# The input projection of a decoder layer as seven block products, with one order of events for all engines

## The reference

```
h = rms_norm(x, norm1_g) * (1 + scale1) + shift1          # 1024 features
proj = h @ w_in                                            # 1024 x 2560
q, k, v, u, vg = split(proj)                               # 512 columns each
q = rms_norm(q per head of 64, q_norm_g); k = rms_norm(k per head, k_norm_g)
u = gelu(u); vn = rms_norm(gelu(vg) per group of 128, v_norm_g)
o_mlp = u * (tril(w_s) @ vn per chunk of 128 tokens + b_s)
```

## Time and profile before

| what | value |
|---|---|
| median of 3 runs | 3535.37 us (3531.87 to 3537.59) |
| profiled execution | 3530.1 us, span 3528.4 us |
| TensorE busy over the span | 3294.7 us (93%) |
| DVE, ACT, POOL busy | 1684.9, 1080.3, 1494.9 us |
| mean granted TensorE clock | 0.97 of full speed |
| bytes moved | 536.85 MB, 152 GB/s |

### The profile page before, as it was taken

One profiled execution on the slowest core, in us unless ns is written; L12 is line 12 of the kernel. 1 busy time (PEld: TensorE's weight loads), 2 busy tenths in 40 slices (PEclk: granted clock), 3 DMA queues, 4 the chain that ended last, 5 costly groups with the idle time before them and its releaser, 6 DMA issues.

```text
span 3528.4 us, 52997 instructions
## 1 busy us (share of the span) xinstructions
PE 3294.7 (93%) x17710; PEld 2288.5 (65%) x17711; DVE 1684.9 (48%) x2542; ACT 1080.3 (31%) x2337; POOL 1494.9 (42%) x1222
## 2 busy tenths in 40 slices
PE   4799999989999959999998999998999999899999
PEld 1344444436656637777776777776777778777777
DVE  0211212138878825554543553544555354566565
ACT  0221222238889812322210331220232121132220
POOL 0010110126656625554533654543555454565553
PEclk8899999989999979999999999999999999999999
DMA  8411101020110056777777667778677674322222
GB/s 327 164 33 59 54 30 49 30 82 2 49 50 14 2 186 213 247 236 242 254 250 274 210 228 245 235 243 267 220 237 241 225 242 154 103 79 77 72 84 78
DMA packets 237935, 536.85 MB, mean 152 GB/s; under 512 B 26831, under 2 KB 60351, under 8 KB 217705
## 3 DMA queue, kind: packets, MB, share of 16 engines
q1 hardware_dynamic: 207081, 361.36, 31.2%
q10 hardware_dynamic: 30592, 172.24, 13.9%
HBM read 498.96 MB, written 34.55 MB: 151 GB/s over the span
## 4 chain that ended last, share of the span: by engine, by line
PE 54%; DVE 6%; issue 2%; DMA 1%; ACT 1%; SPq 0%; DVEq 0%; ACTq 0%
PE ff_pB L1392 46%; PE s_pZ L962 3%; PE s_pO L976 3%; DVE ff_conv L1672 1%; DVE s_left L1038 1%; DMA ff_act_in<-scratch_catT 1%; DVE ff_x L1599 0%; DVE ff_act_in L1688 0%; PE s_pZ L968 0%; DVE s_stop L1042 0%; ACT ff_conv L1470 0%; DVE ff_conv L1674 0%; DVE ff_rs L1681 0%; DMA s_kpage<-in_cache_k 0%; DVE s_kpage L1665 0%
## 5 line engine op out<-in xcount | busy, mean ns | idle before, releaser
L1392 PE MATMUL ff_pB<-ff_act_in,ff_w 128*128 128x256 f32 (+1 forms) x2496 | 616.3, 391 | 38.4 <-DMA ff_act_in<-scratch_catT 18.4
L1392 PEld LDWEIGHTS ff_pB<-ff_act_in,ff_w 128*128 128x128 f32 x2496 | 474.2, 193 | 150.6 <-issue 64.7
L1727 POOL TENSOR_TENSOR ff_sums<-ff_w 128x512 f32<-128x512 f32 (+1 forms) x152 | 191.4, 1259 | 755.1 <-PE ff_pB L1392 609.6
L417 PE MATMUL in_pA<-in_w,in_hT 128*128 128x512 f32 (+1 forms) x1024 | 449.2, 594 | 1.0 <-DVE in_hT L536 1.0
L1672 DVE SCALAR_TENSOR_TENSOR ff_conv<-ff_raw,k_vecT,ff_conv 128x512 f32<-128x512 f32 x352 | 381.7, 1085 | 84.4 <-ACT ff_raw L1477 78.2
L1392 PE MATMUL ff_pB<-ff_diff_up,ff_sums 128*128 128x256 f32 (+1 forms) x1600 | 391.0, 387 | 26.7 <-DVE ff_x L1599 22.7
L1599 DVE SCALAR_TENSOR_TENSOR ff_x<-ff_pB,k_mod,ff_x 128x256 f32<-128x256 f32 (+2 forms) x448 | 213.9, 480 | 385.2 <-PE ff_pB L1392 382.1
L856 POOL TENSOR_TENSOR at_stop<-at_stop,at_left 128x512 f32<-128x512 f32 (+3 forms) x320 | 311.5, 999 | 181.4 <-ACT at_stop L796 176.0
L1500 ACT ACTIVATE ff_raw<-ff_pB 128x256 f32<-128x256 f32 (+1 forms) x352 | 136.0, 388 | 778.9 <-PE ff_pB L1392 772.9
L1392 PEld LDWEIGHTS ff_pB<-ff_diff_up,ff_sums 128*128 128x128 f32 x1600 | 301.8, 191 | 92.1 <-DVE ff_x L1599 23.5
L1648 DVE TENSOR_TENSOR ff_raw<-ff_raw,ff_pB 128x256 f32<-128x256 f32 (+1 forms) x264 | 111.4, 424 | 483.4 <-PE ff_pB L1392 483.3
(11 more groups left out here) (187 smaller groups left out, 4711.2 us busy)
## 6 DMA issues: line engine op xcount, KB each, us to landing
ff_w<-in_w_units ACTq DMA_DIRECT2D x136, 1024.0 KB, 6.0
s_kpage<-in_cache_k SPq DMA_DIRECT2D x512, 256.0 KB, 3.9
s_vpage<-in_cache_v SPq DMA_DIRECT2D x512, 256.0 KB, 3.1
wada<-in_w_ada SPq DMA_DIRECT2D x8, 3072.0 KB, 11.5
ff_w<-in_w_units ACTq DMA_DIRECT2D x16, 768.0 KB, 5.3
in_w<-in_w_in SPq DMA_DIRECT2D x5, 2048.0 KB, 19.4
in_x<-in_x_prompt SPq DMA_DIRECT2D x16, 512.0 KB, 5.3
ff_act_in<-scratch_catT SPq DMA_DIRECT2D x4, 2048.0 KB, 14.5
```

What stands on the lines that cost most here:

```text
L417: last = pe.matmul(pA[0:R, m % 2, :], hT[:, kt, t * R:(t + 1) * R], w[:, kt, col:col + DSB], start=kt == 0, stop=kt == KT - 1)
L1392: last = pe.matmul(into, left[:, kt * P:(kt + 1) * P], right[:, kt, :], start=kt == 0 and p in (1, 2, 5), stop=kt == depth(j) - 1, skip_gr ...
L1727: pool.tensor_tensor(S3, A11, A21, ALU.subtract).then_inc(sums_ready, 1)
```

## The change

x comes as columns (`x_cols`, features on partitions, already an input of the last stage), so that the transposes of x go. The 2048 tokens are taken as 8 pairs of tiles. The root mean square is a sum over partitions: ACT squares half of the features of a pair (`nsq`), POOL folds 8 slices to 2 (`fold`), TensorE multiplies by ones (`stat`), and after both halves ACT takes the root, DVE the reciprocal (`invert`), POOL multiplies (`scale`), ACT modulates (`modulate`). All of this but the multiplication and sums runs a pair ahead.

For u, gate, q and k a pair's 256 x 1024 by 1024 x 512 product is cut into 2 x 2 blocks (token tile by half of the features; half of the features by half of the columns) and made of seven products of four 256-column matmuls each. Sums of token blocks (`sums`, POOL) are made for each pair; differences of weight blocks (`tdiff`, DVE) once, one of them in place of a weight block. Products 1, 6, 7, 4 add up in one PSUM bank and 2, 5, 3 in another; ACT copies products 1, 6, 5, 4 to SBUF as they stand in the bank (`take`), DVE adds 2, 7 and 3 to those copies (`add`). v stays as two banks of 512 columns for each pair. u has tokens on partitions now; `om` adds `b_s` and multiplies with u in one DVE instruction per tile and group, in place, and is transposed by TensorE (`turn`) before its store. Norm, square and gain work on two tiles (1024 columns) at once. The samples come between the seventh and the eighth pair and use plain products. One list of events (`in_events`) gives every engine its order; the loops are unrolled. `w_in` loads in the order u, gate, q, k, v; the `k_wd` copies stand behind the loads; `b_s` is loaded as a column for each token of a chunk.

```diff
-IN_COLUMNS = {"q": 0, "k": DSB, "u": 3 * DSB, "g": 4 * DSB, "v": 2 * DSB}
+IN_COLUMNS = {"u": 3 * DSB, "g": 4 * DSB, "q": 0, "k": DSB, "v": 2 * DSB}
...
+            "hT": ctx.enter_context(nc.sbuf_tensor("in_hT", [P, 2, KT, 2 * P], F32)),
+            "hs": ctx.enter_context(nc.sbuf_tensor("in_hs", [P, KT, S], F32)),
...
-            small(k["bs"][:].rearrange("p g c -> p (g c)"),
-                  a["b_s"][0].rearrange("g (a c) -> a (g c)", a=1).to_broadcast([P, G * P]))
+            small(k["bs"][:], a["bs_cols"])
+            for b in range(NSEQ):
+                small(k["bs_s"][TS * b:TS * b + TS, :], a["bs_cols"][0:TS, :])
...
+            x_cols = a["x_cols"].rearrange("(t p) q -> p t q", p=P)
+            sp.dma_start(nxt["hT"][:, 0, :, :], x_cols[:, :, 0:2 * P]).then_inc(nxt["x_loaded"][0], 16)
+            for kind, col in IN_COLUMNS.items():
+                src = a["w_in"][0].rearrange("(t p) n -> p t n", p=P)[:, :, col:col + DSB]
+                sp.dma_start(nxt["w"][:, :, col:col + DSB], src).then_inc(nxt["w_loaded"][kind], 16)
+                if kind == "u":
+                    sp.dma_start(nxt["hs"][:], x_cols[:, :, SEQ:SEQ + S]).then_inc(nxt["xs_loaded"], 16)
+                    sp.dma_start(nxt["hT"][:, 1, :, :], x_cols[:, :, 2 * P:4 * P]).then_inc(nxt["x_loaded"][1], 16)
             sp.wait_ge(ws_masked, 2)
             for b in range(NSEQ):
                 sp.dma_start(wd[TS * b:TS * b + TS, :, TS * b:TS * b + TS], wsT[0:TS, :, 0:TS]).then_inc(wd_loaded, 16)
-            for t in range(TT):
-                sp.dma_start(nxt["x"][:, t, :], a["x_prompt"][0, t * P:(t + 1) * P, :]).then_inc(nxt["x_loaded"][t], 16)
-            for kind, col in IN_COLUMNS.items():
-                src = a["w_in"][0].rearrange("(t p) n -> p t n", p=P)[:, :, col:col + DSB]
-                sp.dma_start(nxt["w"][:, :, col:col + DSB], src).then_inc(nxt["w_loaded"][kind], 16)
-            sp.wait_ge(small_loaded, 16 * (14 + 4 * TS))
+            sp.wait_ge(small_loaded, 16 * (14 + NSEQ + 4 * TS))
             sp.wait_ge(wd_loaded, 16 * NSEQ)
...
+def in_events():
+    events = [("nsq", 0, 0), ("fold", 0, 0), ("stat", 0, 0), ("nsq", 0, 1), ("fold", 0, 1), ("stat", 0, 1), ("root", 0), ("invert", 0),
+              ("scale", 0), ("modulate", 0), ("sums", 0), ("tdiff", "u")]
...
+                   *once(("tdiff", "q"), ("invert", SAMPLE)), m("g", 6), *ahead(("nsq", 0), ("fold", 0)), m("g", 5), *ahead(("stat", 0)),
...
+                   m("k", 7), ("hnorm", p, "q"), ("om", p), *ahead(("modulate",)), m("k", 3), ("turn", p, "om")]
...
+IN_ADDED = [product for product in IN_PRODUCTS if product[2] in (2, 7, 3)]
+IN_TAKEN = [product for product in IN_PRODUCTS if product not in IN_ADDED]
+def in_bank(p, kind, part):
+    second = part in (2, 5, 3) or (kind == "v" and part == 1)
+    return 2 * (IN_UNITS.index((p, kind)) % 2) + second
...
+            def multiply(p, kind, part):
+                product = (p, kind, part)
+                R, bank = size(p), pB[in_bank(*product)]
+                B11, B12, B21, B22 = weights_of(kind)
+                if IN_EARLIER[product]:
+                    drained(pe, IN_EARLIER[product])
+                if p in (0, SAMPLE) and part in (1, 0, "s"):
+                    pe.wait_ge(w_loaded[kind], 16)
...
+                A11, A12, A21, A22 = tokens_of(p)
+                S1, S2, S3, S4 = (ss[:, n, :, :] for n in range(4))
+                if kind == "u" and part in (1, 2):
+                    pe.wait_ge(h_ready, KT * p + (halfk if part == 1 else KT))
+                if kind == "u" and part == 6:
+                    pe.wait_ge(sums_ready, 4 * p + 4)
+                if kind == "v":
+                    for kt in range(KT):
+                        last = pe.matmul(bank[:], hT[:, p % 2, kt, P * part:P * part + P], w[:, kt, IN_COLUMNS["v"]:IN_COLUMNS["v"] + DSB],
+                                         start=kt == 0, stop=kt == KT - 1)
+                    last.then_inc(prod_done, 1)
+                    return
+                if p == 0 and part in (6, 7, 4):
+                    pe.wait_ge(diffs_ready, 4 * (IN_KINDS.index(kind)) + {6: 3, 7: 3, 4: 4}[part])
+                T2, T3, T4 = (tw[kind][:, n, :, :] for n in range(3))
+                left, right = {1: (A11, B11), 2: (A12, B21), 6: (S2, T2), 5: (S1, B12), 7: (S3, T3), 3: (S4, B22), 4: (A22, T4)}[part]
+                for kt in range(halfk):
+                    last = pe.matmul(bank[:, 0:HC], left[:, kt, :], right[:, kt, :], start=kt == 0 and part in (1, 2, 5), stop=kt == halfk - 1,
+                                     skip_group_check=part in (6, 7, 4, 3))
+                last.then_inc(prod_done, 1)
...
+                elif name == "stat":
+                    p, half = which
+                    if roots_before(p):
+                        pe.wait_ge(rooted, roots_before(p))
...
+                    else:
+                        pe.wait_ge(folded, 2 * nth("fold", p, half))
+                        last = pe.matmul(pS[:, 0:2 * P], k["ones"][:], sq[:, 0:2 * P], start=half == 0, stop=half == 1)
+                    last.then_inc(statted, 1)
...
+                elif name == "turn":
+                    p, use = which
+                    R = size(p)
+                    if use == "om":
...
+                        pe.wait_ge(gained, nth("gain", p, "k"))
+                    for t in range(tiles(p)):
+                        turn_waits((p, use, t))
+                        src = raw["u" if use == "om" else use]
+                        for r in range(HP):
+                            last = pe.transpose(pX[turn_bank((p, use, t))][:, r * R:(r + 1) * R], src[0:R, t, r * P:(r + 1) * P], k["ident"][0:R, 0:R])
+                        last.then_inc(turn_done, 1)
...
+            def take(p, kind, part):
+                product = (p, kind, part)
...
+                bank, into = pB[in_bank(*product)], raw[kind]
+                act.wait_ge(prod_done, prod(product))
...
+                    t, half = {1: (0, 0), 6: (0, 1), 5: (1, 1), 4: (1, 0)}[part]
+                    dst, src = into[:, t, HC * half:HC * half + HC], bank[:, 0:HC]
+                act.activation(dst, src, ACT.Copy).then_inc(taken, 1)
...
+                elif name == "nsq":
+                    p, half = which
+                    if IN_AT[event] > 1:
+                        act.wait_ge(statted, IN_AT[event] - 1)
+                    if reduced_before(event):
+                        act.wait_ge(hss_ready, reduced_before(event))
...
+                    else:
+                        act.wait_ge(x_loaded[p % 2], 16 * (p // 2) + 16)
+                        src = hT[:, p % 2, halfk * half:halfk * half + halfk, :].rearrange("p t q -> p (t q)")
+                        act.activation(sq[:], src, ACT.Square).then_inc(squared, 1)
...
+            def add(p, kind, part):
+                product = (p, kind, part)
+                t, half, ahead = {2: (0, 0, 1), 7: (1, 1, 5), 3: (0, 1, 6)}[part]
+                dve.wait_ge(prod_done, prod(product))
+                drained(dve, (p, kind, ahead))
+                dst = raw[kind][:, t, HC * half:HC * half + HC]
+                dve.tensor_tensor(dst, dst, pB[in_bank(*product)][:, 0:HC], ALU.add).then_inc(added, 1)
...
+                elif name == "tdiff":
+                    kind, n = which[0], 4 * IN_KINDS.index(which[0])
+                    B11, B12, B21, B22 = weights_of(kind)
+                    T2, T3, T4 = (tw[kind][:, i, :, :] for i in range(3))
+                    dve.wait_ge(w_loaded[kind], 16)
+                    for i, (into, one, two) in enumerate(((T3, B22, B12), (B12, B12, B11), (T2, B22, B12), (T4, B21, T2))):
+                        if i:
+                            dve.wait_ge(diffs_ready, n + i)
+                        dve.tensor_tensor(into, one, two, ALU.subtract).then_inc(diffs_ready, 1)
...
+                    tile = raw[kind][0:R, 0:tiles(p), :].rearrange("p n (h e) -> p (n h) e", e=e)
+                    dve.tensor_tensor(tile, tile, hrstd[0:R, 0:n].unsqueeze(2).to_broadcast([R, n, e]), ALU.mult).then_inc(normed, 1)
+                elif name == "om":
+                    p, R = which[0], size(which[0])
+                    bs = k["bs_s"] if p == SAMPLE else k["bs"]
+                    dve.wait_ge(gelued, nth("gelu", p, "u"))
+                    for t in range(tiles(p)):
+                        dve.wait_ge(turn_done, TURN_AT[p, "mix", t])
+                        for g in range(G):
+                            u = raw["u"][0:R, t, g * P:g * P + P]
+                            ins = dve.scalar_tensor_tensor(u, pX[turn_bank((p, "mix", t))][0:R, g * P:g * P + P], bs[0:R, g:g + 1], u, ALU.add, ALU.mult)
+                        ins.then_inc(om_ready, 1)
...
+                if name == "fold":
+                    pool.wait_ge(squared, nth("nsq", *which))
+                    pool.tensor_tensor(sq[:, 0:4 * P], sq[:, 0:4 * P], sq[:, 4 * P:8 * P], ALU.add).then_inc(folded, 1)
```

(72 more changed lines are left out.)

614 lines of the change are left out of this document (289 added, 325 removed).

## The result

The changed kernel takes 3569.52 us (median of 4 runs, 3565.23 to 3571.39); the kernel before, beside it, 3533.68 (3531.87 to 3537.59). The ratio is 1.0096, 95% interval 1.0081 to 1.0110. The forecast was 3543 with a range up to 3563: the direction was right, the size was too small by 26.5 us, and the time lies outside the range. The profiled execution has a span of 3569.7 us, 41.3 more than the one before.

What follows compares the result with a forecast made beforehand. TensorE's count of matmul columns was taken as the bound. 143.3 + 580.6 + 35.6 + 1.0 + 4.4 = 764.9 against 757.08, 7.8 us later, gave 3538 profiled and 3543 as median; own range 3534 to 3553, with rivals 3518 to 3563.

Steps and rivals of the forecast that it cites:

- start at full pace: Time from which TensorE runs as if at full pace: 24.8 us after the barrier (bounds 21 and 29), at 143.3.
- (a): TensorE's wait in front of the `om` transposes, for DVE's chain behind k7: 2.7 us in each of eight pairs.
- (b): TensorE's wait in front of the next pair's column sum, behind g6 and g5: 2.0 us, seven times.
- first pair's extra: An extra table load in the first pair, costing 1 us.
- tail: Stage end, from the last v through transposes, copies and last store to the attention's first load: 4.4 us.
- The barrier: Before the projection: `k_wd` copies behind all x and w loads delay its start to 118.5, 17 us later.
- The longer chain: Stage start: the first pair's dependent norm, scale, modulation and sums take 28.1 us; full pace counts from 24.8 after the barrier.
- The products: TensorE's work: products 1.73 us apart, 66.4 us per pair, samples 43.4, column sums 6.0; 580.6 us in all.
- The forecast's own sign: Sign in the new profile that the forecast is wrong: products standing further apart than 1.8 us.
- the waits were not covered: Denies the faster rival: DVE and ACT keep ahead, the pairs' 35.6 us of waits go, 3507 us; chance 0.2.
- the barrier was held: Denies the no-change rival: copies land beside queued weights, start 4.8 us earlier, 3538 us; chance 0.1.
- Clearly slower: Rival: POOL's second scale instruction holds DVE's normalisation of q, 2.5 us per pair, 20 us, 3563; chance 0.2.

Runs made afterwards that it cites:

- the copies early: Changed kernel with the block of `ws_masked` and the eight `k_wd` copies put back ahead of the x and w loads: 3558.6 us, 1.0051 of the kernel before.
- both moves: Changed kernel with the `om` transposes behind the first v bank and the next pair's first column sum behind g7: 3512.8 us, 0.9936 of the kernel before.
- om later: Changed kernel with only the `om` transposes moved, behind the first v bank instead of in front of it: 3533.7 us, 0.9990 of the kernel before.

## Why the prediction was right in kind and wrong in size

| step | forecast | measured |
|---|---|---|
| stage begins | 118.5 | 116.23 |
| start at full pace | 143.3 | 139.9 (-3.4) |
| work of TensorE without waits and falls | 580.6 | 586.6 (+6.0) |
| waits (a) and (b), first pair's extra | 36.6 | 33.3 (-3.3) |
| lower clock behind the waits | 0 | 20.3 (+20.3) |
| tail | 4.4 | 5.9 (+1.5) |
| attention's first load | 764.9 | 785.97 (+21.1) |

Of the 26.5 us by which the forecast missed the median, 21.1 lie ahead of this load; the other 5 lie behind it, inside the scatter. The rows other than the lower clock add up to +0.8 us, which is luck: each is off by 1.5 to 6.0 and their signs cancel.

*The barrier* was right: copies behind the loads hold it. The bounds were 113.7 to 124; with the copies early it is 107.55.

*The longer chain*: 23.7 us instead of 24.8. POOL's two scale instructions took 6.47 (forecast 7.1, bounds 5.1 and 10).

*The products* are 1.73 us apart as forecast. The work as a whole was 6.0 too small: a pair without waits takes 67.6 (67.80 with 0.20 of wait, from the run with both moves) where the sum gave 66.4 + 0.86; that is 2.7 in eight pairs. The column sum of the samples (1.7) was not counted, and the samples' group took 44.0 instead of 43.4. 1.0 us is not placed.

*The two waits*: place, cause and number were right, and their parts too. DVE behind k7 in the second pair:

```profile
270.40 0.42 DVE L700 TENSOR_TENSOR in_raw_k<-in_raw_k,in_pB 128x256 f32<-128x256 f32 x1 [2.66 <-PE in_pB L524]
270.74 0.25 DVE L741 RECIPROCAL in_hrstd<-in_hroot 128x16 f32<-128x16 f32 x1
271.02 1.23 DVE L744 TENSOR_TENSOR in_raw_q<-in_raw_q,in_hrstd 128x1024 f32<-128x1024 f32 x1
272.17 2.15 DVE L753 SCALAR_TENSOR_TENSOR in_raw_u<-in_pX,k_bs,in_raw_u 128x128 f32<-128x128 f32 x8
```

0.42, 0.25, 1.23 and eight times 0.27, against 0.42, 0.2, 1.22 and 0.26. **The step that failed is the price of these waits**, "8 x 2.7 + 7 x 2.0 = 35.6 us": a wait was priced at its own length, and the lower clock behind it was put at nothing without a reason. In this stage, where TensorE is the bound, an idle piece cost its length and in most cases also the slower work behind it. Both together were 33.3 + 20.3 = 53.6. The two moves of the order leave 3.1 us of waits, so 50.5 should go, and 52.2 went from product 3 to the load (the 0.2 us in each pair seen with "om later" make up the rest). The forecast's own sign, products further apart than 1.8 us, shows it: 3.23 behind the column sum in the second pair.

The trace of before had two rows for it. One is the clock of 0.54 where TensorE does nothing, which I used for the start alone. The other I overlooked: the 0.99 of the earlier trace rows is 1.00 from 145 to 726 us and 0.50 from 726.8 to 740.5, right behind an idle piece of 1.73 us in the samples. The 48 matmul records of 32 columns that follow it take 10.45 us, 0.22 each, where the 16 ahead of it took 0.12 each. The row of that piece, and the window of 50 us around it:

```profile
L433 PE MATMUL in_pT<-k_ident,in_kn 32*128 32x32 f32 x4 | 0.6, 284 | 1.7 <-POOL in_kn L614 1.7
700.00:750.00 50.00, 47.23 (x155) 22.95 (x154) 5.46 (x11) 7.74 (x16) 2.44 (x3) 0.86 0.09 25
```

None of my rivals was "the clock". Two slips in the forecast's sums change nothing: 0.24 and 0.1 make 0.34 and not 0.33, and POOL's terms up to the normalisation of q add up to 13.5 us and not 13.7.

*The tail*: store to load took 4.0 us instead of 2.44; not tried.

*The rivals*: the waits were not covered, the barrier was held, and POOL does not hold up DVE's normalisation of q: it takes 1.23 us in every pair, as long as the others. "Clearly slower" thus had a time that lay nearer to the result, by a cause that did not occur. The Trainium skill (SBUF — State Buffer, Who interferes with whom) says that a DVE instruction with two SBUF inputs and a GpSimd instruction that reads SBUF exclude each other. Where the two do meet, at the start, this case's rows agree: DVE's subtraction takes 3.24 us beside POOL's scale and 1.23 alone, and the scale takes 6.47 beside DVE and 4.63 alone.

What was spent, seen from the result: the change does save TensorE work. With the same products, hardly a wait and the copies early the kernel is 0.9% faster than before; two places in the order of events cost 53.6 us, and the place of eight small copies 8.9 (785.97 to 777.12).
